# Gate and up products leave PSUM in their own order, and the fold products pick every fourth column

## The chip, the cores and the metric

The kernel runs on one core of a Trainium2 chip. The metric is the device time of one execution in microseconds; less is better. The core's engines work side by side and meet at semaphores: TensorE (PE) multiplies, VectorE (DVE), ScalarE (ACT) and GpSimd (POOL) compute elementwise, and SyncE (SP) issues most of the transfers.

## The reference, cut to what matters

The program is one decoder layer on 320 tokens (256 of a prompt, 64 of a sample), width 1024, all in fp32. A mixer stage comes first, then a mixture of 32 experts with two experts per token, then a gated embedding term and a norm. The change is inside the experts:

```
for e in range(N_EXPERTS):
    h = jax.nn.silu(x @ w_eg[e]) * (x @ w_eu[e])      # (tokens, 1024) -> (tokens, 512)
    out = out + combine[:, e:e + 1] * (h @ w_ed[e])   # (tokens, 512) -> (tokens, 1024)
```

## The kernel before

The experts are taken in 16 pairs, a and b. For each expert a gather brings up to 48 token rows (SLOTS) into `xg`, and the rows are turned by TensorE so that they can be the stationary operand. The weights of an expert are three matrices of 2 MB (gate, up, down), and they stream through `ring`, six slots of 2 MB, one for each matrix of a pair. SP issues one load per slot as soon as the slot is free.

A full-precision product is made out of faster ones. Each matrix is cut in 12 "units" per pair (two per matrix). For a unit ScalarE writes the rounded weights `hi` (L945), VectorE writes the rest `lo` (L1294), and TensorE multiplies three of four blocks with `hi` and `lo` (L768, L769) and the fourth in plain fp32 straight from `ring` (L771). The stationary operand has the rounded part of the tokens in columns 0 to 47 and the rest in columns 64 to 111, so a product in PSUM has two row groups that have to be added.

Units 0 to 3 are gate and up of expert a, 4 and 5 the down matrix of the expert before it (b of the pair before), 6 to 9 gate and up of b, 10 and 11 down of a. `copy_gu` (L948 to L955) is ScalarE's copy of a finished gate or up product, 128 rows by 512 hidden columns, from PSUM to `gu`. `turn_hidden` (L775 to L784) is a group of eight products on TensorE that does two things at once: it takes 128 of the 512 hidden columns as the stationary operand, so the result is turned with hidden columns on partitions, and it multiplies by `fold`, a 128x48 matrix with ones at rows s and s + 64, so the two row groups are added. An fp32 product is two load and multiply pairs in the trace, so a group has 16 of each. The down weights are laid out so that partition p holds rows 4p to 4p + 3; therefore product j has to take hidden columns 4q + j.

The copy now does this sorting: it reads PSUM in order and writes element 4q + j of a row to place (j, q), neighbours 128 fp32 (512 bytes) apart. The stationary operand of L783 then is 128 fp32 that lie side by side.

The order of work is written out by hand in a `step` for each engine. TensorE comes to `turn_hidden(x)` before unit 6 and to `turn_hidden(x + 1)` at the end of the round. It waits there for both copies (`gu_copied`). On ScalarE the copies stand between weight splits: copy of gate, split of units 6 and 7, copy of up, split of units 8 and 9, and in the same way for expert b. A split waits for its weights (`raw_in`) and for a free `hi` buffer (`unit_done`). After `turn_hidden` ScalarE applies silu (L960), and VectorE multiplies and splits the result into `hr` (L1302 to L1306).

Other places where a stationary operand is read with a step: `turn_rows` (L829, recorded at L572) takes `h` at steps of 8 fp32, 32 bytes; the turning of the token features (L600, also at L572, tile `mixT`) takes steps of 2 fp32, 8 bytes; `pick_slots` (L740) takes 48 bf16 of `sel` at steps of 32, 64 bytes. `perm` is turned from packed columns.

Of the kernel before, what the change touches and what calls it, by code (L numbers as in the profile page):

```python
# [25 lines left out]
ACT = mybir.ActivationFunctionType  # L26
AX = mybir.AxisListType
F32 = mybir.dt.float32
# [5 lines left out]
P = 128  # L34
# [39 lines left out]
def need(eng, sem, value):  # L74

    if not (isinstance(value, int) and value <= 0):
        eng.wait_ge(sem, value)
# [13 lines left out]
def build(nc, x_prompt, x_sample, state_pool, p_prompt, p_sample, g_mix, w_in, w_pool, pool_scale,  # L91
# [4 lines left out]
    with ctx:  # L96
        ctx.enter_context(nc.allow_non_contiguous_dma(reason="small transposed weights"))

        def sem(name):
            return ctx.enter_context(nc.semaphore(name))  # L100
# [16 lines left out]
        def sb(name, shape, dt=F32, stack=ctx):  # L117
            return stack.enter_context(nc.sbuf_tensor(name, shape, dt))
# [7 lines left out]
        fold = sb("fold", [P, SLOTS])  # L126
# [32 lines left out]
        with ExitStack() as experts:  # L159
            hi = sb("hi", [P, HI_RING, SPLIT], F32R, experts)  # L160
            lo = sb("lo", [P, LO_RING, SPLIT], F32R, experts)
            xr = sb("xr", [P, KC, 2, 2, HALF], F32R, experts)
            xz = sb("xz", [P, 2, 2, P], F32, experts)
            h32 = sb("h32", [P, 4, P], F32, experts)
            hr = sb("hr", [P, 4, 2, HALF], F32R, experts)
            gu = sb("gu", [P, 2, 4, P], F32, experts)
            sg = sb("sg", [P, 4, SLOTS], F32, experts)
            yc = sb("yc", [SLOTS, D], F32, experts)
            yo = sb("yo", [SLOTS, D], F32, experts)
# [71 lines left out]
        p_gu, p_t, p_y, p_x = ps[:, 0:2, :], ps[:, 2, :], ps[:, 3:5, :], ps[:, 5:7, :]  # L241
        IDX, FIRST_IDX, LOGITS, LOGIT_ROWS, PLACES = 7, 4, 6, 7, 5
        p_t = p_t[:, 0:2 * 4 * SLOTS].rearrange("p (g j s) -> p g j s", g=2, j=4)
# [3 lines left out]
        def at_half(t, half):  # L247


            return slice(half * NS, half * NS + NS) if t == TILES - 1 else slice(0, P)  # L250

        def halves_by_chunk(t):
# [36 lines left out]
        gu_copied, t_done, silu_done, h_step, hr_ready = (sem(n) for n in (  # L289
            "gate_up_copied", "gate_up_transposed", "silu_done", "hidden_step", "hidden_ready"))  # L290
# [276 lines left out]
        def _(pe):  # L567
            mm = nc.tensor.matmul
# [21 lines left out]
            for g in range(NG):  # L590
                for k in range(KC):
                    last = mm(ps[:, 4 + g, 0:NT], w_a[:, k, g * P:(g + 1) * P], nT[:, k, 0:NT],  # L592
                              start=k == 0, stop=k == KC - 1)
# [33 lines left out]
            for g in range(NG):  # L627
                if g:
                    pe.wait_ge(a_f, g)
                for k in range(KC):  # L630
                    last = mm(ps[:, 3 + g, 0:NT], w_u[:, k, g * P:(g + 1) * P], nT[:, k, 0:NT],  # L631
                              start=k == 0, stop=k == KC - 1)
# [92 lines left out]
            for t in range(TILES):  # L725
                for c in range(t + 1):
                    mm(ps[:, PLACES, t * NE:(t + 1) * NE], before if c == t else ones_b, memb[:, c, :],
                       start=c == 0, stop=c == t)
            for c in range(TILES):
                last = mm(ps[:, PLACES, TILES * NE:(TILES + 1) * NE], ones_b, memb[:, c, :],  # L730
                          start=c == 0, stop=c == TILES - 1)
# [43 lines left out]
            def turn_hidden(x):  # L775

                if isinstance(x, int) and x == 0:
                    pe.wait_ge(ple_f, 6)
                pe.wait_ge(gu_copied, 2 * x + 2)
                need(pe, hr_ready, x)  # L780
                for c in range(2):
                    for j in range(4):
                        done = mm(p_t[:, c, j, :], gu[:, c, j, :], fold[:, :], start=True, stop=True)  # L783
                done.then_inc(t_done, 1)  # L784

            def step(n, i, q, first, last):
                x = (q * PAIRS + i) * 2
                if not last:
                    pe.wait_ge(xr_ready, q * PAIRS + i + 1)
                for u in range(UNITS):  # L790
                    if not has(u, first, last):
                        continue
                    if u == 4:
                        pe.wait_ge(hr_ready, x)
                        pe.wait_ge(y_added, x - 1)
                    if u == 10:
                        turn_x(n + 1)
                        pe.wait_ge(hr_ready, x + 1)
                        need(pe, y_added, x)
                    if not last and u == 6:  # L800
                        turn_hidden(x)
                    multiply(n, u, first, last)
                    if first and u == 3:
                        pick_slots(q, 1)
                if not last:
                    turn_hidden(x + 1)
# [35 lines left out]
            for n, t in enumerate(LAST_ORDER):  # L842
                r = ROWS[t]
                pe.wait_ge(cp2, n + 1)
                for half, k in halves_by_chunk(t):
                    w = ring[:, 3 + k // 4, (k % 4) * D + half * BLOCK:(k % 4) * D + (half + 1) * BLOCK]
                    done = mm(ps[at_half(t, half), 2 * t + half, :], nT[:, k, t * P:t * P + r], w,  # L847
                              start=k == 0, stop=k == KC - 1)
# [7 lines left out]
        def _(act):  # L856
            acti = nc.scalar.activation
# [90 lines left out]
            def copy_gu(n, x, u):  # L948

                c = (u % 6) // 2  # L950
                act.wait_ge(unit_done, n * UNITS + u + 1)
                if c == 0:
                    need(act, t_done, x)
                acti(gu[:, c, :, :].rearrange("p j q -> p q j"),  # L954
                     p_gu[:, c, :].rearrange("p (q j) -> p q j", j=4), ACT.Copy).then_inc(gu_copied, 1)  # L955

            def silu(x):
                act.wait_ge(t_done, x + 1)
# [3 lines left out]
            def step(n, i, q, first, last):  # L962
# [6 lines left out]
                if not first:  # L969
                    copy_gu(n - 1, x - 1, 9)  # L970
# [26 lines left out]
                if not last:  # L997
                    copy_gu(n, x, 1)
                    high(6, 7)
                    copy_gu(n, x, 3)  # L1000
                    high(8, 9)
# [464 lines left out]
```

## Time and profile before

| what | value |
|---|---|
| median of 3 runs | 738.64 us (738.35 to 740.05) |
| the profiled execution | 740.69 us, span 738.9 us |
| mean granted TensorE clock | 0.966 |
| TensorE matmul busy | 703.5 us, 95% of the span |
| VectorE, ScalarE busy | 500.4 us (68%), 443.0 us (60%) |
| expert loop, 16 rounds | about 160 to 680 us, a round 31.18 us |
| DMA | 232.88 MB, 315 GB/s over the span |

The span is from the first to the last instruction, and the profiled execution's time has 1.8 us around it. Busy times of engines overlap. A round is one pass over a pair of experts; it shows best between two fold groups of the same kind.

### The profile page before, as it was taken

Reading aid. Unit: us, or ns where it says so; the run is one execution under the profiler, and the core shown is the slowest. Engines: PE = TensorE matmul, PEld = TensorE weight load, DVE = VectorE, ACT = ScalarE, POOL = GpSimd, SP = SyncE. Lnnn points to the kernel's source line nnn. Section 1 sums busy time; section 2 is a strip of 40 time slices with the busy share of each in tenths; the row PEclk is TensorE's granted clock in tenths of the full one; section 3 lists DMA queues with packets and bytes.
Section 4 is the critical chain, followed back from the end, with each engine's and each line's share of the span. In section 5 each row is a group of like instructions: output and inputs, shape, how many; then the busy total and the mean of one; then the engine's idle time right before and its main releaser. Section 6 shows DMA issues by size and latency. Waiting matters only on the chain.

```text
span 738.9 us, 9217 instructions
## 1 busy us (share of the span) xinstructions
PE 703.5 (95%) x2932; PEld 470.8 (64%) x2932; DVE 500.4 (68%) x586; ACT 443.0 (60%) x438; POOL 144.7 (20%) x168
## 2 busy tenths in 40 slices
PE   2999999799999999999999999999999999999895
PEld 2646644448677777677777777777777776775342
DVE  5164014663779797797977978779787797873543
ACT  3013102343778787787877778777787686872153
POOL 4000000122313122131321312213122220311000
PEclk9999889787999999999999999999999999999998
DMA  9983030708899999999999999999999999974401
GB/s 273 371 320 114 22 114 28 271 12 342 292 404 388 430 407 414 415 386 425 406 419 404 397 424 403 403 410 391 426 410 410 394 412 416 382 282 174 144 14 57
DMA packets 30347, 232.88 MB, mean 315 GB/s; under 512 B 8168, under 2 KB 9512, under 8 KB 17520
## 3 DMA queue, kind: packets, MB, share of 16 engines
q1 hardware_dynamic: 22221, 226.43, 77.0%
q0 software_dynamic: 4480, 5.26, 2.2%
q10 hardware_dynamic: 3626, 0.94, 0.6%
q8 instruction: 10, 0.16, 0.1%
q14 instruction: 10, 0.07, 0.0%
HBM read 231.15 MB, written 9.32 MB: 325 GB/s over the span
## 4 chain that ended last, share of the span: by engine, by line
PE 82%; DMA 9%; DVE 4%; ACT 2%; issue 2%; POOL 1%; SPq 0%; DVEq 0%; POOLq 0%; ACTq 0%
PE ps L771 20%; PE ps L768 16%; PE ps L769 16%; PE ps L783 7%; DMA ring<-in_w_eg_dram 6%; PE ps L678 5%; PE ps L847 5%; PE ps L592 3%; PE ps L572 2%; PE ps L617 2%; PE ps L631 2%; DMA xg<-hn_rows,cur 1%; PE ps L740 1%; DVE perm L1067 1%; DMA ring<-moe_rows 1%
## 5 line engine op out<-in xcount | busy, mean ns | idle before, releaser
L1294 DVE TENSOR_TENSOR lo<-ring,hi 128x1536 fp32r<-128x1536 f32 x192 | 333.1, 1753 | 65.3 <-PE ps L771 45.8
L945 ACT ACTIVATE hi<-ring 128x1536 fp32r<-128x1536 f32 x192 | 280.7, 1484 | 86.4 <-PE ps L771 62.9
L768 PE MATMUL ps<-hi,xr 128*128 128x512 f32 x384 | 193.0, 503 | 0.0
L769 PE MATMUL ps<-lo,xr 128*128 128x512 f32 x384 | 151.4, 394 | 0.0
L771 PE MATMUL ps<-ring,xz 128*128 128x512 f32 x256 | 130.8, 592 | 0.0
L768 PE MATMUL ps<-hi,hr 128*128 128x512 f32 x192 | 96.5, 502 | 1.6 <-DVE hr L1306 1.6
L768 PEld LDWEIGHTS ps<-hi,xr 128*128 128x128 f32 x384 | 72.6, 189 | 35.5 <-issue 20.6
L769 PEld LDWEIGHTS ps<-lo,xr 128*128 128x128 f32 x384 | 72.8, 190 | 34.0 <-issue 23.1
L522 POOL DMA_INDIRECT moe_rows<-yo,cur x32 | 50.2, 1569 | 192.4 <-DVE yo L1284 192.4
L954 ACT ACTIVATE gu<-ps 128x512 f32<-128x512 f32 x64 | 69.1, 1080 | 29.5 <-PE ps L771 29.5
L769 PE MATMUL ps<-lo,hr 128*128 128x512 f32 x192 | 75.9, 395 | 0.0
L783 PEld LDWEIGHTS ps<-fold,gu 128*128 128x128 f32 x512 | 63.5, 196 | 17.0 <-issue 14.0
L771 PE MATMUL ps<-ring,h 128*128 128x512 f32 x128 | 66.2, 598 | 0.0
L783 PE MATMUL ps<-fold,gu 128*128 128x48 f32 x512 | 62.1, 276 | 1.4 <-ACT gu L954 1.4
L518 POOL COPY cur<-row_out 48x1 int32 (+1 forms) x32 | 36.9, 1154 | 127.8 <-DMA moe_rows<-yo,cur 127.8
L771 PEld LDWEIGHTS ps<-ring,xz 128*128 128x128 f32 x256 | 48.5, 190 | 10.7
L768 PEld LDWEIGHTS ps<-hi,hr 128*128 128x128 f32 x192 | 36.4, 189 | 19.1 <-issue 11.4
L769 PEld LDWEIGHTS ps<-lo,hr 128*128 128x128 f32 x192 | 36.5, 190 | 17.0 <-issue 11.5
L1284 DVE TENSOR_TENSOR yo<-ps,yc 48x1024 f32<-48x1024 f32 x32 | 38.7, 1209 | 7.3 <-ACT yc L934 7.3
L509 POOL DMA_INDIRECT xg<-hn_rows,cur x34 | 36.3, 1066 | 20.1 <-POOL cur L504 14.9
L934 ACT ACTIVATE yc<-ps 48x1024 f32<-48x1024 f32 x32 | 32.7, 1022 | 9.8 <-PE ps L771 9.1
L847 PE MATMUL ps<-ring,nT 128*128 128x512 f32 (+1 forms) x96 | 36.8, 634 | 1.0 <-DVE nT L1380 1.0
(212 smaller groups left out, 573.3 us busy)
## 6 DMA issues: line engine op xcount, KB each, us to landing
ring<-in_w_eg_dram SPq DMA_DIRECT2D x32, 2048.0 KB, 14.3
ring<-in_w_eu_dram SPq DMA_DIRECT2D x32, 2048.0 KB, 14.7
ring<-in_w_ed_dram SPq DMA_DIRECT2D x31, 2048.0 KB, 15.3
ring<-in_w_in_dram SPq DMA_DIRECT2D x3, 2048.0 KB, 18.0
ring<-in_w_out_dram SPq DMA_DIRECT2D x2, 2048.0 KB, 22.9
ring<-in_w_ple_gate_dram SPq DMA_DIRECT2D x2, 2048.0 KB, 9.7
ring<-in_w_ed_dram SPq DMA_DIRECT2D x2, 1024.0 KB, 8.5
ring<-moe_rows SPq DMA_DIRECT2D x4, 512.0 KB, 6.6
```

The lines of the kernel that those rows point to most:

```text
L518: nc.gpsimd.tensor_copy(cur[:, 2:3], row_out[:, bass.ds(i, 1)]).then_inc(cur_out, 1)
L522: nc.gpsimd.indirect_dma_start(moe_rows, bass.IndirectOffsetOnAxis(cur[:, 2:3].bitcast(U32), 0), yo[:, :], None, bounds_check=2 * NT - 1, ...
L678: last = mm(ps[at_half(t, half), h_bank[t] + half, :], mixT[:, k, t * P:t * P + r], w, start=k == 0, stop=k == KC - 1)
L768: mm(out, parts, hi[:, u % HI_RING, cut], start=begin, stop=False)
L769: done = mm(out, parts, lo[:, u % LO_RING, cut], start=False, stop=end)
L771: done = mm(out, z, ring[:, slot, blk * BLOCK:(blk + 1) * BLOCK], start=begin, stop=end)
L783: done = mm(p_t[:, c, j, :], gu[:, c, j, :], fold[:, :], start=True, stop=True)
L847: done = mm(ps[at_half(t, half), 2 * t + half, :], nT[:, k, t * P:t * P + r], w, start=k == 0, stop=k == KC - 1)
L945: acti(hi[:, u % HI_RING, :], ring[:, u // 2, off:off + SPLIT], ACT.Copy).then_inc(hi_ready, counted(u, first, last))
L954: acti(gu[:, c, :, :].rearrange("p j q -> p q j"), p_gu[:, c, :].rearrange("p (q j) -> p q j", j=4), ACT.Copy).then_inc(gu_copied, 1)
L1284: V.tensor_tensor(yo[:, :].rearrange("p (b n) -> p b n", b=2), p_y[0:SLOTS, :, :], yc[:, :].rearrange("p (b n) -> p b n", b=2), ALU.add).t ...
L1294: V.tensor_tensor(lo[:, u % LO_RING, :], ring[:, u // 2, off:off + SPLIT], hi[:, u % HI_RING, :].bitcast(F32), ALU.subtract).then_inc(lo_r ...
```

## The change

The copy keeps the order of PSUM, so `gu` holds the 512 hidden columns as they came. Each fold product takes its 128 columns by a step of four fp32, 16 bytes, from `gu`. Sizes, counts, semaphores and the order of instructions are the same.

```diff
-            gu = sb("gu", [P, 2, 4, P], F32, experts)
+            gu = sb("gu", [P, 2, 4 * P], F32, experts)
...
                 for c in range(2):
                     for j in range(4):
-                        done = mm(p_t[:, c, j, :], gu[:, c, j, :], fold[:, :], start=True, stop=True)
+                        done = mm(p_t[:, c, j, :], gu[:, c, j::4], fold[:, :], start=True, stop=True)
                 done.then_inc(t_done, 1)
...
-                acti(gu[:, c, :, :].rearrange("p j q -> p q j"),
-                     p_gu[:, c, :].rearrange("p (q j) -> p q j", j=4), ACT.Copy).then_inc(gu_copied, 1)
+                acti(gu[:, c, :], p_gu[:, c, :], ACT.Copy).then_inc(gu_copied, 1)
```

## Rows read from the trace of the kernel before

**Rows 1.** The page: busy us, share, instructions; TensorE's clock in 40 slices.
```profile
PE 703.5 (95%) x2932; PEld 470.8 (64%) x2932; DVE 500.4 (68%) x586; ACT 443.0 (60%) x438; POOL 144.7 (20%) x168
...
PEclk9999889787999999999999999999999999999998
```

**Rows 2.** Windows of an ordinary and a later round: length, busy us, clock, DMA, GB/s.
```profile
292.25:323.43 31.18, 31.18 (x139) 22.28 (x138) 25.89 (x25) 24.44 (x23) 7.49 (x7) 1.00 1.00 405
...
573.00:605.00 32.00, 31.43 (x138) 22.19 (x138) 25.88 (x25) 23.79 (x22) 8.11 (x7) 1.00 1.00 405
```

**Rows 3.** Waits, 130 to 680 us: us in total, times, longest us.
```profile
ACT hi L945 <- DMA ring<-in_w_ed_dram: 9.3, 7, 2.5
...
PEld ps L783 <- ACT gu L954: 3.1, 2, 1.7
...
PE ps L783 <- ACT gu L954: 1.4, 2, 0.8
```

**Rows 4.** Groups by shape, whole span: busy us, mean ns, idle before.
```profile
L954 ACT ACTIVATE gu<-ps 128x512 f32<-128x512 f32 x64 | 69.1, 1080 | 29.5 <-PE ps L771 29.5
...
L783 PEld LDWEIGHTS ps<-fold,gu 128*128 128x128 f32 x512 | 63.5, 196 | 17.0 <-issue 14.0 <-ACT gu L954 3.1
...
L918 ACT ACTIVATE ple<-ps 128x512 f32<-128x512 f32 x4 | 2.4, 597 | 6.6 <-PE ps L717 6.5
```

**Rows 5.** Timeline of an ordinary fold group and its copy: start us, length us.
```profile
397.99 1.06 ACT L954 ACTIVATE gu<-ps 128x512 f32<-128x512 f32 x1
...
400.02 1.02 PE L771 MATMUL ps<-ring,h 128*128 128x512 f32 x2
...
400.45 0.19 PEld L783 LDWEIGHTS ps<-fold,gu 128*128 128x128 f32 x1 [0.24 <-issue]
...
400.88 1.75 PEld L783 LDWEIGHTS ps<-fold,gu 128*128 128x128 f32 x15 [0.24 <-issue]
...
402.56 0.19 PEld L768 LDWEIGHTS ps<-hi,xr 128*128 128x128 f32 x1
```

**Rows 6.** Timeline of the two late fold groups.
```profile
587.12 1.02 PE L771 MATMUL ps<-ring,h 128*128 128x512 f32 x2
587.61 1.05 ACT L954 ACTIVATE gu<-ps 128x512 f32<-128x512 f32 x1
...
588.71 1.86 PEld L783 LDWEIGHTS ps<-fold,gu 128*128 128x128 f32 x16 [1.40 <-ACT gu L954]
...
590.49 0.19 PEld L768 LDWEIGHTS ps<-hi,xr 128*128 128x128 f32 x1
...
619.14 1.02 PE L771 MATMUL ps<-ring,h 128*128 128x512 f32 x2
...
620.99 1.86 PEld L783 LDWEIGHTS ps<-fold,gu 128*128 128x128 f32 x16 [1.66 <-ACT gu L954]
...
622.77 0.19 PEld L768 LDWEIGHTS ps<-hi,xr 128*128 128x128 f32 x1
```

**Rows 7.** Loads of transposes: ns min/median/max; then timeline of those of h.
```profile
L572 PEld LDWEIGHTS ps<-ident,perm x7: 140/141/143, 123.8 to 124.5; 128*128 128x128 f32 x7
...
L572 PEld LDWEIGHTS ps<-ident,mixT x6: 192/202/211, 38.0 to 39.0; 128*128 128x128 f32 x4, 64*128 64x128 f32 x2
...
L572 PEld LDWEIGHTS ps<-ident,h x7: 187/192/193, 709.4 to 710.0; 128*128 128x128 f32 x7
...
709.36 0.86 PEld L572 LDWEIGHTS ps<-ident,h 128*128 128x128 f32 x7 [0.24 <-issue]
...
710.13 0.30 PEld L847 LDWEIGHTS ps<-ring,nT 128*128 128x128 f32 x2
```

**Rows 8.** Loads of L740: timeline, and windows at full and at half clock.
```profile
169.77 8.08 PEld L740 LDWEIGHTS ps<-tok,win 128*48 128x48 bf16 x96 [0.76 <-issue]
...
171.00:172.00 1.00, 1.00 (x14) 1.00 1.07 459
175.00:176.00 1.00, 1.00 (x14) 0.50 1.01 426
```

## The prediction

> **What bounds the kernel now.** I read five views. The page first: TensorE is busy 95% of the span, at the higher of its two clock levels nearly all the time (9s in the PEclk line), ScalarE 60% [rows 1]. A share over the span says little, so I went to the windows of single rounds of the expert loop: a round is 31.18 us in which TensorE has work for 31.18 us [rows 2], and the rounds between 198.7 and 572.9 us are alike to 0.01 us (twelve windows, one shown). ScalarE has 24.4 us of work in such a round, so it idles 6.8 us. The reader is to see that only what TensorE has to do, or what it is made to wait for, can move this loop; a shorter copy on ScalarE is no gain by itself. Yet DMA is near its limit too: its share is 1.00 at about 405 GB/s [rows 2]. That matters below, since ScalarE now and then waits for weights.
>
> Third, the waits: TensorE's wait for the copy being changed appears in only two places of the whole loop, 3.1 us on the weight-load side and 1.4 us on the matmul side [rows 3]. These are two faces of the same two waits. ScalarE itself waited for the third weight matrix 9.3 us in 7 places, late in the loop [rows 3].
>
> **Part one: the copy L954.** There are 64 copies of 128x512 from PSUM to SBUF, 1080 ns each [rows 4]. They read PSUM in order and write neighbouring elements 512 bytes apart. After the change both sides are in order. The nearest row is L918, the same engine, function, size and direction, with both sides in order: 597 ns [rows 4]. So each copy loses 1080 - 597 = 483 ns, and ScalarE 64 x 0.483 = 30.9 us in all.
>
> Nearly all of it lies beside other work. In an ordinary round the later of the two copies that a fold group needs ends at 397.99 + 1.06 = 399.05 us, and TensorE's first load of the fold group comes at 400.45, its second at 400.88 [rows 5]: 1.4 us spare before the change, 1.9 after. What hides the copy is two units of down projection, about 4.5 us of TensorE. No instruction on DVE, POOL or the DMA queues waits for this copy, and the two weight splits behind it on ScalarE are released by TensorE or by DMA, not by ScalarE's time.
>
> The cover is gone in two rounds. There the gate weights of the second expert landed late, ScalarE made two splits and only then could copy. Against the ordinary group [rows 5], where the last L771 pair starts 0.86 us before the second fold load (400.02 to 400.88) and the next unit's load follows 1.68 us later (402.56), the first late group has 1.59 and 1.78 us (587.12, 588.71, 590.49) and the second 1.85 and 1.78 us (619.14, 620.99, 622.77) [rows 6]. The excess is 0.83 + 1.09 = 1.92 us. A copy 0.483 us shorter takes 0.48 from each, since it ends 0.05 us before the load starts (587.61 + 1.05 to 588.71) and the next thing late is the weight transfer itself. That is 0.97 us, and 0.95 us of waiting stays.
>
> **Part two: the fold products L783.** The count stays: 32 groups of 8 fp32 products, each two instruction pairs, 512 loads of 128 columns. Nothing is added in waits. What changes is that a load takes every fourth fp32, 16 bytes apart, where it took 128 neighbours. This is the term that decides, because these groups are bound by their loads and not by the multiplying: 15 loads from 400.88 to the next unit's at 402.56 are 112 ns each [rows 5], with only 48 columns to multiply. Every nanosecond more on a load is 0.5 us on the kernel, all of it exposed.
>
> No row loads fp32 at 16 bytes for a matmul. From below: could it be faster? Its elements cover four times as many bytes, and no row here has a spread load faster than a packed one; I take zero. From both sides otherwise, three kinds of row. The transposes of h near the end take their stationary operand at steps of 32 bytes, also 128 fp32 columns: median 192 ns, and a spacing of (710.13 - 709.36)/7 = 110 ns [rows 7]. The fold loads have a mean of 196 and a spacing of 112 ns [rows 4, 5]. So at double the step of this change, a load is as fast as the packed load that it would replace. The transposes of the token features at 8 bytes have a median of 202 ns, 10 ns more [rows 7]; the h rows had idle DMA engines and these did not, which may be the reason. But packed transposes load in 141 ns [rows 7], so spreading does cost 51 ns there, from a base that the packed fp32 matmul load doesn't reach. I read it as: packed transposes fetch two fp32 at a time, spread ones one, and the fp32 matmul load needs no more than one at any step.
>
> Against it stands the load of L740, the only spread load of a plain matmul: 48 bf16 columns 64 bytes apart, 96 of them in 8.08 us, 84 ns each or 1.75 ns a column [rows 8]. As many loads (14) fall in a microsecond at full clock as at half clock [rows 8], so the array doesn't pace it. By that row 128 columns would take 224 ns, (224 - 112) x 512 = 57.3 us more. Its step is four times this one, the h row's twice; its price per column is also that of the copy, (1080 - 597)/512 = 0.94 ns on top of a normal element at a step of 512 bytes. I guess that steps which are a multiple of 64 bytes share this cost, and 16 and 32 don't. I take 0 as the value, from the nearest row, and keep 5.1 us (10 ns x 512, the 8 byte row) and 57.3 us as the other ends.
>
> The Trainium skill speaks against the change here. Its page "SBUF — State Buffer", under Specifications, wants at least two hits in each 16-byte line for full bandwidth and charges each crossing to a new line; at 16 bytes every column is a new line. The h rows cross a line per column as well and load at the packed fp32 pace, so the trace does not agree for fp32 loads; by the rule taken at its hardest, a doubled load, the kernel would land near the last rival below.
>
> **Sum.** The profiled execution took 740.69 us, of which 738.9 are span. 740.69 - 0.97 + 0 = 739.72 us. The median of the runs shown is 2.05 us below the profiled one. That is nearly the 1.92 us of the two late groups, so an undisturbed run may well have neither, and then nothing is won. The gain is between 0 and 0.97 us; I take the middle, 0.5: 738.64 - 0.5 = 738.1 us. Its own range is 736.9 to 739.5. A measurement of this kernel can tell about 0.3%, 2.2 us, from no change.
>
> **The rivals.**
> (a) *Loads a little dearer.* The spread loads meet DMA writes in SBUF, and lose up to 10 ns each as the 8 byte row might say. 738.6 + 5.1 less 0.5 = up to 743.2 us. From 4.3 ns a load it counts as slower. For: DMA is at 1.00 during the loop [rows 2]. Against: the 8 byte row and the h row differ in two things at once.
> (b) *Loads doubled.* L740's price holds for fp32 at 16 bytes. 738.1 + 57.3 = 795.4 us, and about 793 if a load merely doubles (512 x 107 = 54.8 us, with 107 ns from 112 less the group's start). For: L740 is the only spread load outside the transposes. Against: h at 32 bytes.
> (c) *More copies on the path.* ScalarE runs late behind DMA in more groups of an unprofiled run than the two seen; with five of them, 5 x 0.48 = 2.4 us, 736.2 us. For: seven waits for the third matrix alone [rows 3]. Against: only two of them reached TensorE, and the median is below the profiled run.
> (d) *The copy does not get shorter*, as PSUM reads set its pace. Against: L918 reads the same kind of tile. The time would be 738.6 us, no different from the forecast; it is counted with it.
>
> **How the numbers follow.** Forecast with (d) 0.66; (a) 0.12, half of it beyond the bound; (b) 0.17; (c) 0.05, mostly just beyond it. The range from 735.9 to 743.2 us holds the forecast, (a) and part of (c), about 0.8, and leaves (b) out. Faster 0.04, same 0.73, slower 0.23.
>
> **What the changed profile would show.** L954 near 597 ns for 64 copies, ScalarE about 31 us less busy; if it stays near 1080, (d). L783's loads: about 192 ns long and 110 to 112 ns apart confirm part two; 202 is (a), 300 or more is (b), and then the round grows from 31.18 to about 34.8 us and TensorE's share rises. TensorE's wait for L954 goes from 4.5 us in two places to two shorter ones or none. Rounds still at 31.18 us would show that the freed ScalarE time is worth nothing here. What would make the prediction wrong is one number alone, the time of a load at 16 bytes.

## The result and the profile after

The changed kernel takes 809.87 us (median of 4 runs, 807.36 to 816.63) against 739.07 us before (median of 4, 738.35 to 740.05). The ratio is 1.0944, interval 1.0908 to 1.098 (the two medians alone give 1.0958): 9.4% slower, and 70.8 us between the medians. The forecast was 738.1 us with a range from 735.9 to 743.2; rival (b), the doubled load, had 0.17 and 795.4 us.

The page of the changed kernel shows both halves of the change at once: busy time by engine, the clock line in 40 slices, and the groups that answer to [rows 4].

```profile
PE 772.7 (96%) x2932; PEld 541.0 (67%) x2932; DVE 502.1 (62%) x586; ACT 419.4 (52%) x438; POOL 148.4 (18%) x168
...
PEclk9999699878999999999999999989999999998999
...
L783 PEld LDWEIGHTS ps<-fold,gu 128*128 128x128 f32 x512 | 124.2, 327 | 11.2 <-issue 7.5
...
L954 ACT ACTIVATE gu<-ps 128x512 f32<-128x512 f32 x64 | 37.2, 582 | 41.3 <-PE ps L771 41.3
```

The copy went from 1080 to 582 ns, even a little below the 597 ns of L918. The loads went from 196 to 327 ns. The timeline of one fold group, to be held against [rows 5] (some lines between are left out, here and below, where "..." stands):

```profile
519.11 1.02 PE L771 MATMUL ps<-ring,h 128*128 128x512 f32 x2
519.54 4.00 PEld L783 LDWEIGHTS ps<-fold,gu 128*128 128x128 f32 x16 [0.24 <-issue]
519.97 3.70 PE L783 MATMUL ps<-fold,gu 128*128 128x48 f32 x16
...
523.45 0.21 PEld L768 LDWEIGHTS ps<-hi,xr 128*128 128x128 f32 x1
```

From the group's first matmul (519.97, when its second load starts too) the next unit's load (523.45) is reached after 3.48 us, where it was 1.68. In the chain of work that ended last a group of 16 is 3.54 us long, 1.72 before: 221 and 107.5 ns a load. Windows of three rounds, with the same columns as in [rows 2], and one window behind a fold group:

```profile
232.49:267.30 34.81, 34.81 (x138) 26.18 (x136) 26.01 (x25) 23.03 (x23) 8.51 (x8) 1.00 0.96 371
267.30:304.99 37.69, 37.69 (x138) 27.96 (x137) 26.03 (x25) 23.02 (x23) 7.95 (x8) 0.91 0.89 344
342.61:379.07 36.46, 36.46 (x137) 27.04 (x136) 26.01 (x25) 23.03 (x23) 7.73 (x8) 0.95 0.93 353
524.30:527.60 3.30, 3.30 (x7) 1.90 (x6) 0.10 (x1) 0.17 (x1) 0.91 (x1) 0.51 1.02 416
```

The reader is to see two losses. A round at full clock has grown from 31.18 to 34.81 us, 3.63 us for two groups. And some rounds are longer still, by 1.6 or 2.9 us, with a mean clock below 1.00: in them TensorE went for a while at its lower level of 1.2 GHz (the last window, mean clock 0.51, stands for one such stretch). In the loop of before every round from 198.7 to 572.9 us ran at 1.00.

The 15 rounds between the second and the last fold group add up. From first matmul to first matmul they took 668.20 - 198.53 = 469.67 us before and 734.96 - 197.66 = 537.30 us after, 67.6 us more. Of that 15 x 3.63 = 54.5 us are the growth of a round at full clock; seven rounds with the lower clock add 15.0 us; and against it the 1.9 us of the two late groups [rows 6] are gone, since nobody waits for the copy or for weights any longer: no wait of TensorE on the copy is left, and a 2 MB load of expert weights now lands in 7.8 to 10.0 us (medians of the three kinds) where it took 14.3 to 15.3.

The ten stretches at 1.2 GHz in this loop all begin 2.7 to 4.5 us after the first matmul of a slow group, that is within 0.9 us of the group's end on either side.

### The profile page after: what moved, and what is told of

It is laid out like the page before. It is cut to its first block, busy times and chain, and to the rows that moved or that the text cites. A ratio compares the mean times of both kernels' runs of the same rounds, so it can differ in the third digit from the quotient of the medians.

```text
span 806.9 us, 9217 instructions
## 1 busy us (share of the span) xinstructions
PE 772.7 (96%) x2932; PEld 541.0 (67%) x2932; DVE 502.1 (62%) x586; ACT 419.4 (52%) x438; POOL 148.4 (18%) x168
## 2 busy tenths in 40 slices
DMA packets 30346, 232.88 MB, mean 289 GB/s; under 512 B 8167, under 2 KB 9511, under 8 KB 17519
## 4 chain that ended last, share of the span: by engine, by line
PE 92%; DVE 3%; DMA 2%; ACT 1%; issue 1%; SPq 0%; DVEq 0%; POOL 0%; POOLq 0%; ACTq 0%
PE ps L771 21%; PE ps L768 18%; PE ps L769 17%; PE ps L783 14%; PE ps L678 5%; PE ps L847 4%; PE ps L592 2%; PE ps L572 2%; PE ps L617 2%; PE ps L631 2%; PE ps L740 1%; DVE perm L1066 1%; DMA ring<-moe_rows 1%; PE ps L660 1%; PE ps L659 1%
## 5 line engine op out<-in xcount | busy, mean ns | idle before, releaser
L768 PE MATMUL ps<-hi,xr 128*128 128x512 f32 x384 | 201.8, 526 | 0.0
L769 PE MATMUL ps<-lo,xr 128*128 128x512 f32 x384 | 157.2, 409 | 0.0
L771 PE MATMUL ps<-ring,xz 128*128 128x512 f32 x256 | 137.7, 620 | 0.0
L783 PEld LDWEIGHTS ps<-fold,gu 128*128 128x128 f32 x512 | 124.2, 327 | 11.2 <-issue 7.5
L783 PE MATMUL ps<-fold,gu 128*128 128x48 f32 x512 | 118.8, 387 | 0.0
L522 POOL DMA_INDIRECT moe_rows<-yo,cur x32 | 39.3, 1227 | 304.4 <-DVE yo L1283 304.4
L509 POOL DMA_INDIRECT xg<-hn_rows,cur x34 | 56.0, 1647 | 20.1 <-POOL cur L504 14.9
L954 ACT ACTIVATE gu<-ps 128x512 f32<-128x512 f32 x64 | 37.2, 582 | 41.3 <-PE ps L771 41.3
L769 PEld LDWEIGHTS ps<-lo,hr 128*128 128x128 f32 x192 | 36.9, 192 | 17.2 <-issue 11.6
L518 POOL COPY cur<-row_out 48x1 int32 (+1 forms) x32 | 31.8, 995 | 81.2 <-DMA moe_rows<-yo,cur 81.1
L678 PE MATMUL ps<-ring,mixT 128*128 128x512 f32 (+1 forms) x96 | 36.9, 618 | 0.0
```

Source lines behind the costliest of these rows:

```text
L509: nc.gpsimd.indirect_dma_start(xg[e * SLOTS:(e + 1) * SLOTS, :], None, hn_rows, bass.IndirectOffsetOnAxis(cur[:, e:e + 1].bitcast(U32), 0) ...
L522: nc.gpsimd.indirect_dma_start(moe_rows, bass.IndirectOffsetOnAxis(cur[:, 2:3].bitcast(U32), 0), yo[:, :], None, bounds_check=2 * NT - 1, ...
L678: last = mm(ps[at_half(t, half), h_bank[t] + half, :], mixT[:, k, t * P:t * P + r], w, start=k == 0, stop=k == KC - 1)
L768: mm(out, parts, hi[:, u % HI_RING, cut], start=begin, stop=False)
L769: done = mm(out, parts, lo[:, u % LO_RING, cut], start=False, stop=end)
L771: done = mm(out, z, ring[:, slot, blk * BLOCK:(blk + 1) * BLOCK], start=begin, stop=end)
```

## The experiments

**The copy alone.** Loads packed again, in blocks of 128 columns; the down product then pairs them with the wrong weight rows.

```diff
-                        done = mm(p_t[:, c, j, :], gu[:, c, j::4], fold[:, :], start=True, stop=True)
+                        done = mm(p_t[:, c, j, :], gu[:, c, j * P:(j + 1) * P], fold[:, :], start=True, stop=True)
```

> Only the copy is changed; the fold products load 128 packed columns, so they take hidden columns in blocks and the down product pairs them with the wrong weight rows (the output differs, the amount of work doesn't). Theory (the whole loss is the loads): loads back at 192 ns and 112 ns apart, copies at 582 ns, no drop of the clock inside the loop, 737 to 739 us, ratio to before 0.998 to 1.000. Rival (something in the changed copy itself costs, such as ScalarE or VectorE now arriving at a worse moment): above 742 us.

738.31 us against 740.09, ratio 0.9981 (0.9962 to 1.0). The group rows, and TensorE's wait for the copy on the load side, which stood at 3.1 us in [rows 3]:

```profile
L783 PEld LDWEIGHTS ps<-fold,gu 128*128 128x128 f32 x512 | 63.5, 196 | 16.4 <-issue 14.0
L783 PE MATMUL ps<-fold,gu 128*128 128x48 f32 x512 | 62.1, 276 | 0.8 <-ACT gu L954 0.7
L954 ACT ACTIVATE gu<-ps 128x512 f32<-128x512 f32 x64 | 37.3, 583 | 36.2 <-PE ps L771 36.2
...
PEld ps L783 <- ACT gu L954: 2.4, 2, 1.5
```

Taking 32 us of work from ScalarE is worth 0 to 2.8 us; the wait went from 3.1 to 2.4 us on the load side and from 1.4 to 0.7 us on the matmul side. In the profiled executions the two late rounds were 32.02 and 32.28 us before and are 31.51 and 32.21 us here, 0.58 us less together. The theory holds, and the rival that the copy does harm falls.

**The loads alone.** The copy of before, every fourth column loaded from the sorted buffer (the wrong columns, the same work).

```diff
-                acti(gu[:, c, :], p_gu[:, c, :], ACT.Copy).then_inc(gu_copied, 1)
+                acti(gu[:, c, :].rearrange("p (j q) -> p q j", j=4),
+                     p_gu[:, c, :].rearrange("p (q j) -> p q j", j=4), ACT.Copy).then_inc(gu_copied, 1)
```

> The copy is that of before (neighbours 512 bytes apart), the fold products load every fourth fp32, so they take the wrong columns of the sorted buffer; the amount of work is that of the changed kernel. Theory (the whole loss is the loads, the copy is beside other work): 805 to 812 us, loads of 330 ns, as the changed kernel. If the shorter copy gave anything under these slower rounds, this kernel would be more than 1 us above the changed kernel, beyond what the clock's drops scatter.

812.6 us against 740.09, ratio 1.0979 (1.0936 to 1.1021), which overlaps with that of the whole change. The loads have 327 ns. I had taken more than 1 us above the changed kernel, beyond the scatter of the clock, for a gain of the shorter copy, and the median is 2.7 us above. The traces speak against that reading: a round at full clock is 34.81 us in both, and this execution had 13 stretches at the lower clock in the loop where the other had ten. So the loads carry the loss whole, as far as the scatter of the clock lets one see.

**Steps of 1 to 8.** The eight products of a group each with another step, in the loop as before, and so the eight transposes of the gathered rows; behind the loop rows of loads without DMA traffic.

```diff
+                mm(p_t[:, 0, 0, :], flat[:, 0:128], fold[:, :], start=True, stop=True)
+                mm(p_t[:, 0, 1, :], flat[:, 0:255:2], fold[:, :], start=True, stop=True)
...
+                done = mm(p_t[:, 1, 3, :], flat[:, 0:1017:8], fold[:, :], start=True, stop=True)
```

> The eight fold products of a group load 128 fp32 at steps of 1 to 8 elements (4 to 32 bytes), the eight transposes of the gathered rows do the same, and behind the expert loop stand rows of 12 or 24 loads each at steps of 1, 2, 4, 8 and 16 fp32, plain and transposed, and of 48 bf16 at steps of 1, 2, 8 and 32. The values computed are wrong, only durations are read. Theory A (a plain fp32 load costs double as soon as every column is in a new 16-byte line): 192 ns at steps 1 and 2, something between at 3, 330 ns from step 4 on. Theory B (any step but 1 doubles a plain fp32 load): 330 ns from step 2 on. Theory C (banks: only some steps, 4 among them, are dear): 4, 8 and 16 dear, 3, 5 and 7 cheap. For transposes all three have about 140 ns at step 1 and 192 to 202 at steps 2 and 8, as the trace of before had; new is whether step 4 is dearer there. For 48 bf16: A has steps 1 and 2 cheap, 8 and 32 at 84 ns apart; C only 32.

The loads of 128 fp32 columns at steps 1 to 8, one row each, ns min/median/max:

```profile
L788 PEld LDWEIGHTS ps<-fold,gu x64: 187/189/334, 178.4 to 711.7; 128*128 128x128 f32 x64
...
L789 PEld LDWEIGHTS ps<-fold,gu x64: 196/197/333, 178.8 to 711.9; 128*128 128x128 f32 x64
...
L790 PEld LDWEIGHTS ps<-fold,gu x64: 252/261/331, 179.2 to 712.2; 128*128 128x128 f32 x64
...
L791 PEld LDWEIGHTS ps<-fold,gu x64: 317/330/331, 179.6 to 712.6; 128*128 128x128 f32 x64
...
L792 PEld LDWEIGHTS ps<-fold,gu x64: 315/317/320, 180.1 to 713.1; 128*128 128x128 f32 x64
...
L795 PEld LDWEIGHTS ps<-fold,gu x64: 333/334/336, 181.4 to 714.4; 128*128 128x128 f32 x64
```

(Steps 6 and 7 have 318 and 326.) Theory A: 2 elements are as good as free, 3 lie between, from 4 on it is nearly flat. B falls at step 2, C at steps 5 to 7. Behind the loop the loads of a plain product at step 4 take as long, at the lower clock (0.50 from 742 to 747 us) and with no DMA traffic, so neither DMA writes nor the clock make the price:

```profile
L859 PEld LDWEIGHTS ps<-fold,w_ple_sb x24: 329/330/332, 741.9 to 747.3; 128*128 128x128 f32 x24
```

The transposes of the same experiment behind the loop, at steps 4, 8 and 16, all at full clock, and those of the gathered rows in the loop, at steps 1 to 8 in one row:

```profile
L572 PEld LDWEIGHTS ps<-ident,w_ple_sb x9: 211/212/213, 762.8 to 763.8; 128*128 128x128 f32 x9
...
L572 PEld LDWEIGHTS ps<-ident,w_ple_sb x11: 191/193/196, 764.1 to 765.2; 128*128 128x128 f32 x11
...
L572 PEld LDWEIGHTS ps<-ident,w_ple_sb x9: 195/196/197, 765.6 to 766.5; 128*128 128x128 f32 x9
...
L572 PEld LDWEIGHTS ps<-ident,xg x136: 138/214/234, 156.5 to 707.0; 96*128 96x128 f32 x136
```

The middle one of the first three is the row on which the forecast stood, taken apart: a transpose loads 128 fp32 at 32 bytes in 193 ns, a plain product in 334 ns. Between h and L740 it was not the step that made the difference, but the kind of product. The loads of 48 bf16 at steps of 1, 2, 8 and 32 elements (2, 4, 16 and 64 bytes):

```profile
L875 PEld LDWEIGHTS ps<-gu x24: 99/100/102, 766.9 to 767.5; 128*48 128x48 bf16 x24
...
L877 PEld LDWEIGHTS ps<-gu x24: 99/100/102, 767.5 to 768.1; 128*48 128x48 bf16 x24
...
L879 PEld LDWEIGHTS ps<-gu x24: 165/186/188, 768.1 to 770.2; 128*48 128x48 bf16 x24
...
L881 PEld LDWEIGHTS ps<-gu x24: 176/177/180, 770.3 to 772.2; 128*48 128x48 bf16 x24
```

Sixteen bytes cost as much as 64. My guess of banks at multiples of 64 bytes is refuted; the row of L740 had held this change's own price.

**Every second column.** Pairs are written together, and the products load every second fp32. It computes the reference.

```diff
-                        done = mm(p_t[:, c, j, :], gu[:, c, j::4], fold[:, :], start=True, stop=True)
+                        done = mm(p_t[:, c, j, :], gu[:, c, j // 2, j % 2::2], fold[:, :], start=True, stop=True)
...
-                acti(gu[:, c, :], p_gu[:, c, :], ACT.Copy).then_inc(gu_copied, 1)
+                acti(gu[:, c].rearrange("p a (q b) -> p q a b", b=2),
+                     p_gu[:, c, :].rearrange("p (q a b) -> p q a b", a=2, b=2), ACT.Copy).then_inc(gu_copied, 1)
```

> A form between the two kernels that computes the reference: the copy writes pairs of neighbours (8 bytes together, 1024 bytes apart), the fold products load every second fp32. Theory A (lines of 16 bytes): loads stay at 192 ns, 737 to 740 us, no change from before. Theory B (any step): loads of 330 ns and 805 to 812 us as in the changed kernel. The copy costs between 580 and 1080 ns, and under both theories that is worth nothing.

740.63 us against 740.09, ratio 1.0014 (0.9995 to 1.0033). The copy takes 626 ns, nearly the full saving, and the loads have a mean of 200 ns. Step 2 is nearly free, not quite: every round is 31.35 us where it was 31.18, which is 5 ns a load and 2.6 us over 15 rounds, and the late rounds are gone, which gives 1.9 us back. So no loss that can be told from noise, and no gain either.

```profile
L783 PEld LDWEIGHTS ps<-fold,gu 128*128 128x128 f32 x512 | 66.7, 200 | 14.7 <-issue 14.7
...
L954 ACT ACTIVATE gu<-ps 128x512 f32<-128x512 f32 x64 | 40.1, 626 | 39.1 <-PE ps L771 39.1
```

**Fewer columns.** The steps again, with 64 and 96 columns, to see whether the price goes by lines or by load.

```diff
+                mm(p_t[0:64, 0, 0, :], flat[:, 0:64], fold[:, :], start=True, stop=True)
...
+                mm(p_t[0:64, 0, 3, :], flat[:, 0:253:4], fold[:, :], start=True, stop=True)
...
+                mm(p_t[0:96, 1, 1, :], flat[:, 0:381:4], fold[:, :], start=True, stop=True)
```

> The eight fold products load 64, 96 or 128 columns at several steps (values wrong, only durations are read). Theory A in numbers, from the run of steps 1 to 8: a load takes about 100 ns plus the larger of 0.84 ns a column and 1.73 ns for each 16-byte line it touches. So 64 columns: step 1 154 ns, step 2 155, step 3 183, step 4 211. 96 columns: step 1 180, step 4 266. 128 columns at step 4 from an odd element: 321 to 330, as from an even one. Rival (a fixed penalty for a spread load, whatever its length): 64 columns at step 4 would take about 154 + 138 = 292 ns.

64 columns at steps 1, 3 and 4, then 96 columns at step 4:

```profile
L782 PEld LDWEIGHTS ps<-fold,gu x64: 132/136/227, 177.8 to 677.6; 128*64 128x64 f32 x64
...
L784 PEld LDWEIGHTS ps<-fold,gu x64: 165/174/224, 178.2 to 677.8; 128*64 128x64 f32 x64
L785 PEld LDWEIGHTS ps<-fold,gu x64: 201/214/223, 178.4 to 678.0; 128*64 128x64 f32 x64
...
L787 PEld LDWEIGHTS ps<-fold,gu x64: 252/272/280, 179.1 to 678.6; 128*96 128x96 f32 x64
```

211 and 266 were expected at step 4 and 214 and 272 measured; the fixed penalty would have given 292 for 64 columns. 128 columns from an odd element at step 4 have 330, too. The packed loads came out 18 ns shorter than my formula (136 for 154, 162 for 180) and steps 2 and 3 of 64 columns 15 and 9 ns shorter, so its base of 100 ns fits only the loads with every column in a new line. For those the price goes by the number of 16-byte lines touched, about 1.73 ns each (the spacing of 221 ns over 128 lines), and the rival of a fixed penalty falls.

**Groups cut in two.** The same slow loads, the four gate products one unit earlier; it computes the reference.

```diff
-                pe.wait_ge(gu_copied, 2 * x + 2)
+                pe.wait_ge(gu_copied, 2 * x + 1 + cs[-1])
...
-                for c in range(2):
+                for c in cs:
...
+                    if not last and u == 5:
+                        turn_hidden(x, (0,))
+                    if not last and u == 11:
+                        turn_hidden(x + 1, (0,))
...
-                        turn_hidden(x)
+                        turn_hidden(x, (0, 1) if first else (1,))
```

> The changed kernel, with each fold group cut in two: the four gate products go one unit earlier, before unit 5 (and before unit 11), the four up products stay. It computes the reference, with the same slow loads. Theory (what is left beyond the loads is the half-clock periods, which follow a long stretch of loads with few columns multiplied): stretches of 1.8 us instead of 3.6, no half-clock period in the loop, 793 to 797 us. Rival (the periods come from the mean activity of a round, or the rest of the loss is somewhere else): as the changed kernel, 805 to 812 us.

787.13 us against 741.32, ratio 1.0625 (1.0592 to 1.0657), 6 us below what I expected. Every round is 34.54 us, none longer, though the loads have the same 325 ns:

```profile
368.89:403.43 34.54, 34.54 (x137) 26.15 (x136) 26.12 (x26) 23.06 (x23) 7.24 (x8) 1.00 0.97 368
```

So the lower clock is a loss of its own, and it hangs on how the slow loads are strung together. The two ratios are three points apart, of the nine. Not all of that is the clock: in the profiled executions the lower clock was 15.0 us, two points, and a round at full clock is 0.27 us shorter here than the 34.81 of the changed kernel, 4 us over 15 rounds, for a reason that I have not traced.

**Slow groups for expert b only**, **every fold product twice**, and **96 columns in place of 48** ask what about a group brings the clock down.

```diff
+                        cols_g = gu[:, c, j * P:(j + 1) * P] if packed else gu[:, c, j::4]
...
-                        turn_hidden(x)
+                        turn_hidden(x, True)
```

> Expert a's fold groups load packed columns (taking the wrong ones, so the output differs), expert b's every fourth fp32. Theory (each slow group costs 16 x 0.114 = 1.8 us, plus 1.6 us for each half-clock period): 737 + 29 = 766 us without such periods, up to 774 with as many per slow group as in the changed kernel. Rival (the groups of the two experts differ, one of them having slack): well off 766 to 774.

783.9 us, ratio 1.0574 (1.055 to 1.0598): a miss, 10 us over the upper end. A round at full clock is 33.00 us, 31.18 + 1.82 as it should be. But 12 of the 15 rounds are longer, by 16.4 us together, so half the slow groups cost as much lower clock as all of them. The 12 stretches begin 2.7 to 3.8 us after the first matmul of a slow group, none after a group of packed loads. The loss is not proportional to the slow groups.

```diff
-                        done = mm(p_t[:, c, j, :], gu[:, c, j, :], fold[:, :], start=True, stop=True)
+                        for _ in range(2):
+                            done = mm(p_t[:, c, j, :], gu[:, c, j, :], fold[:, :], start=True, stop=True)
```

> The kernel before with every fold product made twice, packed loads: a group then lasts 3.5 us like a slow one, but with twice the columns multiplied in it. It computes the reference. Loads alone: 739 + 32 x 16 x 0.1075 = 794 us. If the half-clock periods come from how little is multiplied per time, there are none more than before and the time is 794; if they come from the length of a stretch of short products whatever its rate, 805 to 812 us.

This is the kernel before with twice the products. 801.11 us, ratio 1.081 (1.0781 to 1.0839), in between the two ends. Rounds are 34.76 us, and only two of 15 are longer, by 1.6 us each.

```diff
-                        done = mm(p_t[:, c, j, :], gu[:, c, j::4], fold[:, :], start=True, stop=True)
...
+                        else:
+                            done = mm(ps[:, 7, 0:96], gu[:, c, j::4], ident[:, 0:96], start=True, stop=True)
```

> The changed kernel, but all groups except the first multiply 96 columns of the identity into a PSUM bank that nothing reads, with the same slow loads; the fold and the turning are left out, so the output differs. The loads set the pace, so the group should last as long. If the half-clock periods come from how little is multiplied per time, they go and the time is 793 to 797 us; if a long stretch of loads brings them, 805 to 812 us. If 96 columns were to set the pace, the spacing of the loads would rise above 221 ns.

796.88 us, ratio 1.0735 (1.07 to 1.0771). All groups but the first leave the fold and the turning out. The group is as long as with 48 columns, and its loads have 327 ns, but two rounds are longer instead of seven. TensorE's loop in this kernel and then in the changed one, with the mean clock:

```profile
180.00:745.00 565.00, 563.50 (x2156) 0.99 0.91 347
```
```profile
180.00:745.00 565.00, 563.50 (x2126) 0.96 0.90 345
```

With the loads the same, more columns multiplied bring most of the clock back, and groups cut in two bring all of it back. That is shown; which groups exactly are followed by the lower clock, and why the kernel with half of them had as much of it, stays open.

**Down weights in another order.** With hidden row 128 j + p at partition p, neither copy nor load has to sort, and the reference is computed.

```diff
-                        w_ed[0].rearrange("e (p j) n -> e p (j n)", j=4)]
+                        w_ed[0].rearrange("e (j p) n -> e p j n", j=4)]
...
-                        done = mm(p_t[:, c, j, :], gu[:, c, j::4], fold[:, :], start=True, stop=True)
+                        done = mm(p_t[:, c, j, :], gu[:, c, j * P:(j + 1) * P], fold[:, :], start=True, stop=True)
```

> The reorder is gone from both the copy and the loads: the copy is in order, the fold products load packed columns in blocks of 128, and the down weights come with hidden row 128 j + p at partition p, so a partition's 16 KB of them are four pieces of 4 KB in DRAM. It computes the reference. Theory (the copy was hidden, the loads are back at 112 ns): 736 to 739 us, ratio 0.996 to 1.000. Rival (the down weights' transfers are slower in 4 KB pieces, and DMA at a share of 1.00 has nothing to spare): TensorE waits for weights in the second half of the loop, over 745 us.

743.12 us against 740.92, ratio 1.0041 (1.002 to 1.0063). Neither end as I put it: slightly slower. In the waits from 190 to 680 us, ScalarE's waits for the down weights doubled against the 9.3 us of [rows 3]:

```profile
ACT hi L950 <- DMA ring<-in_w_ed_dram: 18.5, 10, 3.0
...
PEld ps L788 <- ACT gu L959: 5.6, 5, 1.5
```

A packed load and a plain copy together gain nothing. The rounds up to 509 us are 31.18 us, those after it up to 33.2. What costs is the layout of the down weights: the kernel with the copy alone does the same work with the old layout and had 0.9981 (0.9962 to 1.0), clear of this one's interval. Here there are 42506 DMA packets instead of 30346, and a 2 MB load of expert weights lands in 15.8 to 17.2 us, 14.8 to 15.9 with the copy alone. None of the versions that compute the reference beats the kernel before.

## Why the prediction was wrong

**The copy.** Right in its length and in being hidden. 483 ns a copy were forecast and 498 measured. "ScalarE about 31 us less busy" was 32 us in the copy's own group, but 23.6 us for the engine (443.0 to 419.4): before, a long copy and the instruction after it overlapped in the record by some 0.2 us, and that counts once. The gain of 0 to 0.97 us is not contradicted by the 0 to 2.8 us of the copy alone; its profiled execution had 0.58 us of it, 0.51 in the first late round and 0.07 in the second, so "0.48 from each" held for one of the two. The 4.5 us of waiting that the prediction names at its end counts the same two waits twice (3.1 and 1.4 us).

**The load.** Wrong, and this is the step that failed: "I take 0 as the value, from the nearest row". The term that was put at 0 measured (221 - 107.5) x 512 = 58.1 us. The nearest row by step was a transpose. The row of the same kind of product, L740, gave 57.3 us as the far end. That 57.3 came so close to 58.1 is in part luck: that 48 bf16 and 128 fp32 have nearly the same price a column (84 ns for 48, 221 ns for 128) no row showed beforehand. I put it away with a guess about multiples of 64 bytes that no row showed, and asked for the step where I should have asked for the kind of instruction. A sign stood in [rows 7] itself: packed transposes load in 141 ns and packed plain products in about 192, so the two kinds don't load alike, and a pace of one can't be carried over to the other. I explained that gap away, by a guess that transposes fetch two fp32 at a time, which no run shows.

The rule of the Trainium skill, page "SBUF — State Buffer", under Specifications, at least two hits in each 16-byte line, is what the plain products follow: step 2 has two hits and takes 197 ns, step 4 has one and takes 330. I had held the transposes against it, and the doubled load that I worked out under it is rival (b), which the prediction calls the last. The trace agrees with the rule for plain products, and is not well described by it for transposes, where steps of 4 and 16 elements stay at 212 and 196 ns.

**The sum.** Rival (b) was right in its mechanism, its place and the length of a round (34.8 us forecast, 34.81 measured), and short by 14 us in the total (795.4 for 809.87). The missing term is the lower clock, 15.0 us in the profiled execution. I took TensorE's rate as given, though a group made twice as long by its loads also multiplies half as much per microsecond. That this brings the clock down is borne out by the runs with 96 columns and with the groups cut in two; the run with half of the slow groups shows that it is not the whole account.

**The other rivals.** (a), a few ns from DMA traffic, has no support: steps 1 and 2 in the full loop have 189 and 197 ns, and step 4 has 330 ns with DMA traffic and without. (c), a gain of 2.4 us from more late groups, is not settled: the profiled execution of the kernel before has two late groups and no more, but the 0 to 2.8 us of the copy alone reach that far. (d) is refuted by the 582 ns.

## What to carry to other kernels

Where a sort has to happen between PSUM and a stationary operand, do it in the copy if the copy has cover: its price there was at most 0.5 us for each of 64 copies on an engine with slack, while on the load side each of 512 loads paid 0.11 us on the engine that sets the pace. If the operand of a plain product must be spread, keep two fp32 in each 16 bytes. And when a cost is bounded by rows, take the row with the same kind of instruction before the row with the nearest size.

## What the runs showed of the hardware

- A load of the stationary operand for a plain product costs about 1.73 ns for each 16-byte line it touches once that exceeds its packed pace (221 ns from load to load for 128 lines, 107.5 packed). The loads themselves last 330 ns for 128 fp32 at steps of 16 bytes, 214 for 64, 186 for 48 bf16. It doesn't hang on the clock: 330 ns at full clock in the loop and at 1.2 GHz behind it, and 84 ns apart for L740 at either level [rows 8].
- Transposes load 128 spread fp32 in 193 to 212 ns at steps of 16, 32 and 64 bytes, and no step up to 32 bytes took them over 234 ns in the loop. Why they escape the price is open.
- A ScalarE copy of 128x512 from PSUM takes 1080 ns when neighbours are written 512 bytes apart, 626 in pairs 1024 bytes apart, 582 in order.
- After fold groups of 3.5 us with 48 columns multiplied every 221 ns, the clock fell to 1.2 GHz ten times in 15 rounds, each time within 0.9 us of a group's end, and cost 15.0 us. With 96 columns multiplied two rounds of 15 were longer; cutting the groups in two kept the loop at 2.4 GHz throughout.
